# Differential attention: six rows in sixteen have their second map scaled and added on GpSimd

## What is computed

```python
def blk(qp, q1b, q2b):
    mask = _chunk_mask(qp, kpos)
    dist = jnp.abs(qp[:, None] - kpos[None, :]).astype(f32)
    bias = jnp.where(mask[None], -slopes[:, None, None] * dist[None], NEG)
    s1 = jnp.einsum('bhqd,bhkd->bhqk', q1b, k1).astype(f32) * scale + bias
    s2 = jnp.einsum('bhqd,bhkd->bhqk', q2b, k2).astype(f32) * scale + bias
    a = jax.nn.softmax(s1, axis=-1) - lam * jax.nn.softmax(s2, axis=-1)
    return jnp.einsum('bhqk,bhkv->bhqv', a.astype(v.dtype), v)
```

## Time and profile before

| | before |
|---|---|
| median of 3 runs | 2593.06 us (2592.95 to 2593.47) |
| the profiled execution: its own time | 2592.49 us |
| its span, first to last instruction | 2590.7 us |
| PE busy over the span | 98% |
| DVE, ACT, POOL busy over the span | 62%, 47%, 14% |
| granted TensorE clock, mean | 0.997 of full speed |
| differential attention | from 430 to 800 us of the span |

### The profile page before, as it was taken

One profiled execution on the slowest core, in us unless ns is written; L12 is line 12 of the kernel. 1 busy time (PEld: TensorE's weight loads), 2 busy tenths in 40 slices (PEclk: granted clock), 3 DMA queues, 4 the chain that ended last, 5 costly groups with the idle time before them and its releaser, 6 DMA issues.

```text
span 2590.7 us, 35438 instructions
## 1 busy us (share of the span) xinstructions
PE 2531.3 (98%) x12188; PEld 2106.7 (81%) x12188; DVE 1614.8 (62%) x3499; ACT 1212.5 (47%) x2183; POOL 352.3 (14%) x432
## 2 busy tenths in 40 slices
PE   8999999999999999989999999999999999999997
PEld 7998888777667999978877888888888888888886
DVE  6123306998995776754468777867758465564765
ACT  6112314777765565554544333533335353443544
POOL 2110002222222222210000000000000001121143
PEclk9999999999999999999999999999999999999999
DMA  7334458553332111145677676666655365776787
GB/s 235 120 107 126 127 163 251 147 136 82 95 134 90 38 30 46 42 130 162 194 239 224 208 221 214 219 194 208 191 163 175 118 216 106 178 162 164 200 162 137
DMA packets 329501, 398.62 MB, mean 154 GB/s; under 512 B 21440, under 2 KB 235728, under 8 KB 321008
## 3 DMA queue, kind: packets, MB, share of 16 engines
q1 hardware_dynamic: 311760, 364.43, 44.8%
q0 software_dynamic: 17568, 31.99, 8.5%
HBM read 239.88 MB, written 156.48 MB: 153 GB/s over the span
## 4 chain that ended last, share of the span: by engine, by line
PE 62%; DVE 3%; DMA 1%; ACT 1%; issue 1%; SPq 1%; POOL 0%; DVEq 0%; ACTq 0%; POOLq 0%
PE ff_ps_x L3284 26%; PE ff_ps_m L3284 13%; PE ff_ps_z L3284 6%; PE ml_ps_s L2158 6%; PE ff_ps_m L1695 4%; PE ml_ps_o L2190 4%; PE ml_ps_t L2172 2%; DMA ml_v_raw<-scr_yT 1%; DMA ff_pieces<-scr_acc 0%; PE ff_ps_r L2721 0%; PE mo_ps_t L2738 0%; SPq L2348 0%; DVE ff_pieces L2451 0%; DVE ff_pieces L2642 0%; DVE ff_pieces L2638 0%
## 5 line engine op out<-in xcount | busy, mean ns | idle before, releaser
L3284 PE MATMUL ff_ps_x<-ff_mv_hi_p,ff_st_hi_p 128*128 128x512 f32 x764 | 297.8, 390 | 0.5 <-ACT ff_u L3024 0.5
L3284 PE MATMUL ff_ps_x<-ff_mv_hi_p,ff_st_lo_p 128*128 128x512 f32 x764 | 297.3, 389 | 0.0
L3284 PE MATMUL ff_ps_x<-ff_mv_lo_p,ff_st_hi_p 128*128 128x512 f32 x764 | 297.3, 389 | 0.0
L2158 PE MATMUL ml_ps_s<-wide,ml_qs 128*128 128x416 f32 (+14 forms) x880 | 194.2, 353 | 4.6 <-PEq L137 2.8
L3130 DVE TENSOR_TENSOR ff_st_lo_p<-ff_ps_m,ff_st_hi_p 128x512 fp32r<-128x512 f32 x190 | 130.5, 687 | 103.4 <-ACT ff_st_hi_p L3007 103.4
L2974 POOL DMA_DIRECT2D scr_acc<-ff_pieces x64 | 55.6, 874 | 1015.2 <-DVE ff_pieces L3154 946.7
L3024 ACT ACTIVATE ff_u<-ff_ps_x 128x512 f32<-128x512 f32 x128 | 76.6, 598 | 214.9 <-PE ff_ps_x L3284 214.9
L3284 PEld LDWEIGHTS ff_ps_x<-ff_mv_hi_p,ff_st_hi_p 128*128 128x128 f32 x764 | 143.4, 188 | 32.6 <-issue 2.0
L3284 PEld LDWEIGHTS ff_ps_x<-ff_mv_hi_p,ff_st_lo_p 128*128 128x128 f32 x764 | 143.4, 188 | 29.8
L3284 PEld LDWEIGHTS ff_ps_x<-ff_mv_lo_p,ff_st_hi_p 128*128 128x128 f32 x764 | 143.4, 188 | 29.6
L2158 PEld LDWEIGHTS ml_ps_s<-wide,ml_qs 128*128 128x128 f32 x880 | 150.4, 188 | 17.1 <-issue 2.9
(11 more groups left out here) (320 smaller groups left out, 6376.0 us busy)
## 6 DMA issues: line engine op xcount, KB each, us to landing
st_raw<-in_w_ff SPq DMA_DIRECT2D x64, 512.0 KB, 6.2
scr_hid<-ff_pieces SPq DMA_DIRECT2D x128, 256.0 KB, 2.6
st_raw<-scr_hid SPq DMA_DIRECT2D x64, 512.0 KB, 5.3
ring<-in_w_ff SPq DMA_DIRECT2D x28, 1024.0 KB, 7.7
scr_t<-ring SPq DMA_DIRECT2D x24, 1024.0 KB, 6.0
ring<-scr_t SPq DMA_DIRECT2D x21, 1024.0 KB, 7.8
scr_acc<-ff_pieces POOLq DMA_DIRECT2D x64, 256.0 KB, 4.0
ring<-scr_u SPq DMA_DIRECT2D x13, 1024.0 KB, 8.2
```

Of the source, the lines that this page charges most:

```text
L2158: m = pe.matmul(ps_s[n % NSB][:, 0:w], q, k, start=j == 0, stop=j == len(pairs) - 1)
L3284: m = pe.matmul(bank[:, :], w[kind][:, k], a[kind][:, k], start=start and k == 0 and i == 0, stop=stop and k == KH - 1 and i == 2, skip_gr ...
```

## The change

In rows 4, 6, 8, 10, 12 and 14 of each head DVE leaves out its last instruction (the one at L1576). In its place POOL gets two. The first, `scale_second`, stands at the row's **end** step: it waits for the second factor (`inv2_step`) and multiplies the second map by it, in place. The second, an addition row = row + second, stands behind the first scaling of the **next** row, and waits for both scalings of its own row. New waits: DVE may write component 1 of row i+2 into the slot of `da_second` only when the sum of row i is made (`pool_summed`); PE's first turn of a group waits for the sums of its even rows too. The other ten rows are as before.

```diff
+        POOL_ROWS = (4, 6, 8, 10, 12, 14)
+        NPR, SUM_INC = len(POOL_ROWS), 1
+        DVE_ROWS = [i for i in range(NT) if i not in POOL_ROWS]
+        NDR = len(DVE_ROWS)
...
+        def pool_sums(h, i):
+            return SUM_INC * (NPR * h + sum(1 for a in POOL_ROWS if a <= i))
...
+        def dve_sums(h, i):
+            return NDR * h + sum(1 for a in DVE_ROWS if a <= i)
...
                 hold(pool, inv_ready, NT * h + i + 1)
                 pool.tensor_scalar(row(i, u), row(i, u), inv[:, i % 2, 0:1], 1.0, ALU.mult, ALU.mult).then_inc(first_scaled, 1)
-
-            heads(pool, {"scale": scaled})
+                if i - 1 in POOL_ROWS:
+
+                    pool.wait_ge(first_scaled, NT * h + i)
+                    pool.wait_ge(second_scaled, pool_sums(h, i - 1))
+                    pool.tensor_tensor(row(i - 1, u), row(i - 1, u), comp_row(i - 1, 1, u), ALU.add).then_inc(pool_summed, 1)
+
+            def scale_second(h, i, u, **at):
+
+                if i in POOL_ROWS:
+                    hold(pool, inv2_step, 2 * (NT * h + i) + 2)
+                    pool.tensor_scalar(comp_row(i, 1, u), comp_row(i, 1, u), inv2[:, i % 2:i % 2 + 1], 1.0,
+                                       ALU.mult, ALU.mult).then_inc(second_scaled, 1)
+
+            heads(pool, {"scale": scaled, "end": scale_second})
...
+                if c == 1 and k0 == 0 and ((i - 2) % NT) in POOL_ROWS and not (first_head and i < 2):
+
+                    dve.wait_ge(pool_summed, pool_sums(h, i - 2))
...
+                if i in POOL_ROWS:
+                    return
                 dve.wait_ge(inv2_step, n + 2)
                 dve.wait_ge(first_scaled, NT * h + i + 1)
...
-            dve.wait_ge(probs_ready, NT * H)
+            dve.wait_ge(probs_ready, NDR * H)
+            dve.wait_ge(pool_summed, SUM_INC * NPR * H)
...
                 if t == 0:
-                    pe.wait_ge(probs_ready, NT * h + 4 * g + 4)
+                    pe.wait_ge(probs_ready, dve_sums(h, 4 * g + 3))
+                    if any(i // 4 == g for i in POOL_ROWS):
+                        pe.wait_ge(pool_summed, pool_sums(h, 4 * g + 3))
```

More of the change, by code:

```diff
@@ L1204, in attention @@
         inv2_step = mem.sem("da_inv2_step")
+        second_scaled, pool_summed = mem.sem("da_second_scaled"), mem.sem("da_pool_summed")
         pT_ready, pv_done = mem.sem(f"da_pT_ready"), mem.sem("da_pv_done")
```

## The result

| | before | after |
|---|---|---|
| median of the runs | 2593.01 us (4 runs, 2591.72 to 2593.47) | 2608.51 us (4 runs, 2606.24 to 2609.87) |
| the profiled execution | 2592.49 us | 2609.87 us |
| its span | 2590.7 us | 2608.1 us |
| mean granted TensorE clock | 0.997 | 0.991 |

The changed kernel is slower by 15.5 us: ratio 1.006, interval 1.0042 to 1.0077, which is 11 to 20 us. The forecast was 2597.5 us with a range up to 2602, so it is wrong in size; slower was one of its two large chances.

The account below looks back on a forecast made before the run. PE was taken to set the pace, with DVE's relief mostly hidden beside it. Terms of 0.52 + 0.58 + 0 = 1.10 us a head, four times, gave +4.4 on 2593.06: 2597.5 us, range 2591 to 2602.

Parts of the forecast that it names:

- its two large chances: Whole kernel: same at 0.47 and slower at 0.41; faster or slower means by over 0.2%, 5.2 us.
- Rival 1: DVE's odd-row instruction does not stand still beside POOL's addition; -1.46 us a head, 2587.2 us; chance 0.12.
- The wait at 682.86: PE's 0.74 us wait, caused by row 14's instruction, goes, but PE then waits longer at T: no gain.
- the one at 646.94: PE's 0.46 us wait caused by row 9's instruction was to remain; row 8's term 0, bounds -0.45 and +0.35.
- new waiting in row 15: PE was to wait some 0.6 us more for banks in row 15.
- row 12: Row 12's POOL addition holds up row 13's instruction, so row 14's factor comes +0.58 us later a head; bounds 0 and +1.19.
- 1.10 us a head: Sum of the terms for rows 14, 12 and 8: 0.52 + 0.58 + 0, paid in four heads.
- Row 15's first reciprocal is no hindrance: In row 14's chain, this reciprocal was to be ready about 1.3 us behind row 14's factor, not delaying POOL.
- The chain: From row 14's second factor to row 15's instruction end: 10.58 us against 10.06 before, so T moves +0.52 us.
- Rows 4, 6 and 10: PE does not wait there, or POOL's sum is through before the odd row's instruction; 0.
- T: First turn of group 3, waiting for row 15's instruction; its delay against the head before is paid in each of four heads.
- PE's wait at T: The wait at group 3's first turn was to grow from 1.25 us to about 2.5.

Follow-up runs that it names:

- experiment 4: Kernel before, plus a useless POOL addition of two SBUF maps behind row 15's first scaling in each head; 2604.83 us, ratio 1.0043.
- experiment 5: Also spelled extra_set: kernel before, plus three POOL memsets of a dead slot behind row 15's first scaling; 2596.07 us against 2592.98, ratio 1.0012.
- Experiment 3: Changed kernel, plus 24 idle PE transposes (40 in the last head) ahead of group 3's first turn; 2601.61 us, ratio 1.0029.
- sum_first: Changed kernel, with POOL's addition straight behind the second scaling, ahead of the next row's first scaling; 2602.42 us, ratio 1.0035.
- all_but_14: Changed kernel, with POOL taking rows 4, 6, 8, 10 and 12 and row 14 back on DVE; 2597.74 us against 2593.67, ratio 1.0016.
- half: Changed kernel, with DVE summing the first half of the columns in the six rows and POOL the rest; 2590.29 us against 2592.98, ratio 0.9990.
- one_input: Changed kernel, with POOL's additions replaced by a scaling by 1.0, leaving out the second map; 2589.92 us, ratio 0.9984.

## Why the prediction was wrong

What was right: DVE stands still in this form of instruction too, and ends at POOL's end plus its own length less a little (696.76 + 2.37 - 0.21 = 698.92 in row 15; 680.08 + 2.10 - 0.20 = 681.98 in row 13, POOL's addition being 676.29 + 3.79). Rival 1 is dead: experiment 4 has the standstill with a foreign addition, and experiment 5 has none with writes. The wait at 682.86 is gone, the one at 646.94 is still there with 0.45 us, and there are 0.59 us of new waiting in row 15 (682.65 in the changed kernel), all as foretold; row 12 cost 0.62 us a head against +0.58. The additions took 4.29 and 3.79 us against 4.13 and 3.62; the estimate from the Trainium skill (GPSIMD Engine Reference, 3.1 Elementwise), 4.26 and 3.73, was nearer. The change took 37.7 us of instructions from DVE; the standstills gave back (1.82 + 0.89 + 0.49 + 0.29 + 0.08) x 4 = 14.3 of them as busy time, and the groups of that line are down by the rest, from 87.6 to 64.2 us. That the engine's busy time fell by only 15.3 us is not explained by this; of the missing 8 us, 2 are in the chunks' instructions, which are longer in the record.

The prediction had 1.10 us a head and nothing else, 4.4 in all. Three steps failed.

1. **"Row 15's first reciprocal is no hindrance: two chunks behind the factor, about 1.3 us."** It ended 2.65 us behind the factor (687.68 to 690.33), since it waits for ACT's exponential of row 15's first map. In the kernel before that wait couldn't be seen, because DVE was at work on row 14's instruction meanwhile: the instruction that the change removes was its cover. These rows, two of before and one of after, show that the exponential itself is no later:

```profile
680.39 2.01 ACT L1477 ACTIVATE da_rows<-da_rows,da_nmax 128x2064 f32<-128x2064 f32 x1
683.23 0.16 DVE L1563 RECIPROCAL da_inv<-da_total 128x1 f32<-128x1 f32 x1
...
688.04 2.01 ACT L1503 ACTIVATE da_rows<-da_rows,da_nmax 128x2064 f32<-128x2064 f32 x1
```

It begins 0.37 us behind row 14's factor before (680.02) and 0.36 after (687.68). Over the whole stage DVE's idle time ahead of the first reciprocals grew from 2.5 to 14.1 us.

The chain was worked out at 10.58 us and took 11.24 (687.68 to 698.92): +0.71 from the late scaling, +0.17 from the addition, -0.16 and -0.06 from the gaps. With the kernel before at 10.06, row 14 costs 1.18 where 0.52 stood.

2. **"Rows 4, 6 and 10: PE is ahead of DVE there ... or the sum is through before the odd row's instruction; 0".** Row 10's addition runs from 662.02 to 665.23, and row 11's instruction is issued at 664.54. It ends 0.49 us later than by its own length, and right there PE waits for it, at the first turn of group 2: 0.4 us a head. The prediction spoke of T as the only turn that waits, because it was the only one in the list of waits; that of group 2 had been met with hardly any time to spare, as these rows of the timeline before, of DVE and of PE, would have told:

```profile
657.92 1.83 DVE L1576 SCALAR_TENSOR_TENSOR da_rows<-da_second,da_inv,da_rows 128x1552 f32<-128x1552 f32 x1
...
659.91 0.60 PE L1642 MATMUL da_ps_t<-ident,da_rows 128*128 128x128 f32 x4
```

The instruction ends at 659.75, and the turn begins 0.16 us later.

3. **PE's wait at T was taken as costing its own length.** It was forecast at 2.5 us and came to 3.6, and behind it TensorE's clock falls: some 4.8 us in the stage, 3.0 ahead of the last T and 1.8 behind. No term and no rival had the clock. Experiment 3 took this part away, and sum_first put a price on one fall.

With 1.19 + 0.4 + 0.6 + 0.1 = 2.3 us a head in place of 1.10, and the clock's 4.8, the stage has 13.9; the medians are 15.5 apart, with an interval of 11 to 20. What is left lies ahead of the stage and behind it, and part of it is further falls of the clock in the profiled execution, whose cause no run here shows. The term for row 12 was right by its own steps: once the 0.5 us that it inherits is taken off, its addition ends within 0.1 us of where the sum had it.

## What to carry to other kernels

Before you remove an instruction, look at what else ended under its cover, and write down by how much each dependent step was late or early; here the exponential's wait was hidden by the very instruction that went. A long two-input addition on POOL keeps DVE's two-input instructions from starting, so POOL's share of such work must be short and end before the next one of DVE: half a row paid, the whole row cost five times what halving won. And a wait of PE is not paid by its length alone: behind waits of 3.15 to 3.64 us at the first three turns the clock fell in 11 of 12 cases, at about 1 us a fall, so look at the granted clock too.

## What the hardware showed that I had not expected

- At the turns of the first three heads the clock fell behind every wait of 3.63 to 3.64 and 3.15 us, and behind two of three waits of 3.3 us in sum_first (3.34, 3.31; not behind 3.35). It never fell there behind 1.0 to 1.8 us. In the last head a wait of 2.78 us was followed by full speed in the kernel before and by a fall in extra_set (12 transposes in 2.82 us) and, behind 2.79, in all_but_14; 3.14 us by full speed in half (12 transposes in 1.53 us) and 3.13 by a fall in one_input. At the passage to latent attention 2.75 us went both ways as well. The same wait can go either way.
- The exclusion holds in the other direction too. In half, POOL's scaling of 976 columns, issued 0.13 us behind DVE's instruction of 960, takes 2.03 us; by 0.27 us + 0.833 ns a column it would be 1.08. It ends 0.94 us behind DVE's end (678.23).
- The addition with two SBUF inputs on POOL costs 0.22 us + 2.1 ns a column (1602 ns at 656, 4292 at 1936), two and a half times a scaling's 0.833 ns.
